# Parameter planes 0 to 3 of the S5 mixer, moved from the attention stage to the first feed-forward layer

## The reference, cut to what matters

```python
# first block, two layers
for layer in range(2):
    h = rms_norm(x, mix_pre_g[layer])
    m = pool_mixer(...) if layer == 0 else swa_sink_attention(q, kk, vv, sinks) @ w_o     # planes were made here
    x = x + rms_norm(m, mix_post_g[layer])
    f = conv_glu_ffn(rms_norm(x, ffn_pre_g[layer]), w_in, conv_w, conv_b, w_out)          # now in that of layer 0
    x = x + rms_norm(f, ffn_post_g[layer])
# second block: modulated norm, S5 mixer, MLP, then norm, SSD mixer, MLP, final norm
def _s5_mixer(h, w_in, lam_re, lam_im, log_dt, b_re, b_im, c_re, c_im, d, w_glu, b_glu):
    dt = exp(log_dt)[:, None]
    lam_bar = exp(lam * dt)                                    # complex, 64 groups x 64 states
    b_bar = ((lam_bar - 1) / lam)[..., None] * (b_re + i b_im) # 64 x 64 x 16
    c_mat = c_re + i c_im
    ...                                                        # scan over time, y = C h
```

## Time and profile before

| | |
|---|---|
| runs of the kernel before | 2322.3 us median, 2322.2 to 2325.84 (3 runs) |
| profiled execution | span 2324.2 us, the time that the page gives for it |
| PE busy | 99% of the span |
| DVE, ACT, POOL busy | 63%, 45%, 15% |
| PE's granted clock over 40 slices | 9 tenths or more in each |
| DMA, mean | 122 GB/s |

### The profile page before, as it was taken

One profiled execution on the slowest core, in us unless ns is written; L12 is line 12 of the kernel. 1 busy time (PEld: TensorE's weight loads), 2 busy tenths in 40 slices (PEclk: granted clock), 3 DMA queues, 4 the chain that ended last, 5 costly groups with the idle time before them and its releaser, 6 DMA issues. The chain is left out here.

```text
span 2324.2 us, 35082 instructions
## 1 busy us (share of the span) xinstructions
PE 2291.4 (99%) x12994; PEld 1930.6 (83%) x12994; DVE 1474.5 (63%) x2160; ACT 1051.7 (45%) x1728; POOL 348.9 (15%) x379
## 2 busy tenths in 40 slices
PE   9999999999999999999999999999999999999998
PEld 8888888867888888897788888888878789888888
DVE  5785788798688768879554324447578744432433
ACT  6653554556565344654344313325556533421421
POOL 0120121111322212110010000010136621000001
PEclk9999999999999999999999999999999999999999
DMA  5455453232345555544222222223212122232221
GB/s 216 143 183 197 174 184 124 82 116 73 137 168 178 186 167 185 179 186 165 71 77 106 91 106 93 91 82 110 95 56 76 39 91 91 91 106 93 90 93 70
DMA packets 56333, 282.53 MB, mean 122 GB/s; under 512 B 7980, under 2 KB 18992, under 8 KB 28320
## 3 DMA queue, kind: packets, MB, share of 16 engines
q1 hardware_dynamic: 34128, 213.85, 25.8%
q0 software_dynamic: 12560, 58.80, 7.4%
q10 hardware_dynamic: 9536, 8.39, 1.1%
HBM read 265.15 MB, written 15.86 MB: 121 GB/s over the span
## 5 line engine op out<-in xcount | busy, mean ns | idle before, releaser
L2329 DVE TENSOR_TENSOR w_lo<-raw,w_hi 128x1024 fp32r<-128x1024 f32 x386 | 505.4, 1346 | 399.8 <-ACT w_hi L1439 399.6
L1439 ACT ACTIVATE w_hi<-raw 128x1024 fp32r<-128x1024 f32 x386 | 388.8, 1053 | 416.1 <-PE ps L527 401.9
L525 PE MATMUL ps<-h_hi,w_hi 128*128 128x512 f32 (+1 forms) x1304 | 459.6, 352 | 5.2 <-DVE h_lo L2402 1.8
L526 PE MATMUL ps<-h_lo,w_hi 128*128 128x512 f32 (+1 forms) x1304 | 452.1, 347 | 1.6 <-issue 1.6
L527 PE MATMUL ps<-h_hi,w_lo 128*128 128x512 f32 (+1 forms) x1304 | 451.8, 346 | 0.0
L525 PEld LDWEIGHTS ps<-h_hi,w_hi 128*128 128x128 f32 x1304 | 246.9, 189 | 47.8 <-issue 11.3
L526 PEld LDWEIGHTS ps<-h_lo,w_hi 128*128 128x128 f32 x1304 | 247.0, 189 | 32.7 <-issue 2.6
L527 PEld LDWEIGHTS ps<-h_hi,w_lo 128*128 128x128 f32 x1304 | 247.1, 189 | 30.5
L531 PE MATMUL ps<-h_hi,w_hi 128*128 128x512 f32 (+1 forms) x712 | 270.6, 382 | 0.8 <-DVE tv L2828 0.8
L532 PE MATMUL ps<-h_lo,w_hi 128*128 128x512 f32 (+1 forms) x712 | 270.2, 382 | 0.0
L3430 POOL TENSOR_TENSOR sqsum<-sqsum,sq 128x256 f32<-128x256 f32 (+1 forms) x83 | 91.4, 1101 | 958.1 <-issue 588.8
(11 more groups left out here) (463 smaller groups left out, 3490.2 us busy)
## 6 DMA issues: line engine op xcount, KB each, us to landing
raw<-weights_dram SPq DMA_DIRECT2D x161, 1024.0 KB, 4.8
ada_w<-ada_dram POOLq DMA_DIRECT2D x48, 1024.0 KB, 5.1
raw<-weights_dram SPq DMA_DIRECT2D x32, 704.0 KB, 4.0
par<-par_dram SPq DMA_DIRECT2D x8, 1152.0 KB, 6.9
par_dram<-plane POOLq DMA_DIRECT2D x10, 512.0 KB, 3.8
tab<-tab_dram SPq DMA_DIRECT2D x8, 512.0 KB, 7.5
x_tok<-x_rows_dram SPq DMA_DIRECT2D x4, 512.0 KB, 5.5
x<-x_in_dram SPq DMA_DIRECT2D x1, 2048.0 KB, 14.5
```

The lines of the kernel that those rows point to most:

```text
L525: nc.tensor.matmul(dst, w_hi[:, o:o + P], rhs_hi, start=start, stop=False)
L526: nc.tensor.matmul(dst, w_hi[:, o:o + P], rhs_lo, start=False, stop=False)
L1439: nc.scalar.activation(w_hi[:, o:o + TILE // 2], raw[:, o:o + TILE // 2], ACT.Copy).then_inc(w_hi_done, 1)
L2329: nc.vector.tensor_tensor(w_lo[:, o], raw[:, o], w_hi[:, o].bitcast(f32), SUB).then_inc(w_split, 1)
```

## The change

Planes 0 to 3 are now made by DVE in `ffn0_out_b`: two pieces ahead of tile 0, then 3, 3, 3, 3 and 2 pieces behind `split_lo` in tiles 0 to 4 (`PIECES_BEFORE`, `PIECES_AT`). They lie, with their inputs and products, in the memory of `h_hi` and `h_lo`, which is idle in that phase. The constants that they need move one phase group earlier: `constants5` now runs in `ffn0_out_a`, in tiles 2, 4, 5 and 6, and ACT's `decay_functions` in tile 0 of it. Plane 4 stays in attention, in units 8 to 11, in buffers of its own. The stores of planes 0 to 3 are issued by ACT, behind its `squares`; those of plane 4 by POOL, as before. POOL loads `s5_b` and `s5_c` and zeroes the four buffers before its adds of `ffn0_out_b`. DVE waits for the eight stores before `stream_halves(0, ...)`, which overwrites the memory.

```diff
-    PLANE_PIECES = [(n, piece) for n in (1, 2, 3, 4) for piece in range(4)]
+    LAST_PLANE = 4
+    b_h, c_h, prod_h, cross_h = (place(n, D, offset=H0 + 4 * k * KB) for k, n in enumerate(("s5_b_early", "s5_c_early", "prod5_early", "cross5_early")))
+    plane5 = [[place(f"plane{u}{k}", D, offset=H0 + (16 + 8 * u + 4 * k) * KB) for k in range(2)] for u in range(2)]
+    PLANE_PIECES = [(n, piece) for n in range(LAST_PLANE) for piece in range(4)]
+    PIECES_BEFORE, PIECES_AT = 2, (3, 3, 3, 3, 2, 0)
...
# ACT
+        def planes_stored(s):
+            for n, part in parts_of(pieces_by(s - 1) if s else 0, pieces_by(s)):
+                o = (C_AT + (n - 1) * 2 * P if n else B0_AT) + part * P
+                act.wait_ge(sem("plane_im" if part else "plane_re"), n + 1)
+                act.dma_start(par_dram.rearrange("(j p) c -> p j c", p=P)[:, :, o:o + P],
+                              as3(plane5[n % 2][part][:, :], DC)).then_inc(sem(f"plane_stored{n % 2}"), 16)
         def rope_sines(s):
+            planes_stored(s)
...
-                if layer == 0 and half == "b":
-                    decay_functions()
-                    tiles(f"ffn{layer}_out_a", copy_out, (out_chunk, 1), then=transposed5 if layer else None)
+                    tiles(f"ffn{layer}_out_a", copy_out, (out_chunk, 1), then=transposed5 if layer else decay_functions)
...
# DVE
+            for u in range(2):
+                dve.wait_ge(sem(f"plane_stored{u}"), 64)
             stream_halves(0, post, {...
...
         def constants5(s):
-            if s == 0:
+            if s == 2:
                 lambda5()
-            elif s == 1:
+            elif s == 4:
                 powers5()
-            elif s == 2:
+            elif s == 5:
                 coefs5((1, 2))
-            elif s == 3:
+            elif s == 6:
                 coefs5((3, 4))
...
+        def early_planes5(s):
+            for piece in PLANE_PIECES[pieces_by(s):pieces_by(s + 1)]:
+                early5(*piece)
...
-                    tiles(f"ffn{layer}_out_a", nothing, ada=ADA_OUT[layer], then=fold5 if layer else None)
+                    tiles(f"ffn{layer}_out_a", nothing, ada=ADA_OUT[layer], then=fold5 if layer else constants5)
...
-                    tiles(f"ffn{layer}_out_b", add_out, (out_chunk, 1), splits="last", then=more_turns5 if layer else constants5, last=2)
+                    else:
+                        dve.wait_ge(sem("b_landed"), 16)
+                        dve.wait_ge(sem("c_landed"), 16)
+                        for piece in PLANE_PIECES[:PIECES_BEFORE]:
+                            early5(*piece)
+                    tiles(f"ffn{layer}_out_b", add_out, (out_chunk, 1), splits="last", then=more_turns5 if layer else early_planes5, last=2)
...
# DVE in attention
-        dve.wait_ge(sem("b_landed"), 16)
-        for piece in range(4):
-            early5(0, piece)
...
-            early5(*PLANE_PIECES[2 * s - 6])
             weigh(s - 3)
-            early5(*PLANE_PIECES[2 * s - 5])
             soften(s - 2)
...
-            if 8 <= j < 14:
-                early5(*PLANE_PIECES[j + 2])
+            if 8 <= j < 12:
+                early5(LAST_PLANE, j - 8)
...
# POOL
+                if half == "b" and not layer:
+                    gp.wait_ge(tile_done, tile_at(FIRST["ffn0_out_b"] - 1))
+                    gp.dma_start(b_h[:, :], s5_b).then_inc(sem("b_landed"), 16)
+                    gp.dma_start(c_h[:, :], s5_c).then_inc(sem("c_landed"), 16)
+                    for u in range(2):
+                        for k in range(2):
+                            ins = gp.memset(plane5[u][k][:, :], 0.0)
+                    ins.then_inc(sem("pool_set"), 1)
```

More of the change, by code:

```diff
@@ L102 @@
 START = {"mod_kept": 1, "xbc_done": 3}
-POOL_SET = {name: k + 1 for k, name in enumerate(("ones", "planes", "s5", "rows180", "rows181"))}
+POOL_SET = {name: k + 1 for k, name in enumerate(("ones", "planes", "last_plane", "s5", "rows180", "rows181"))}
 def eight(name, n=8):
@@ L229, in build, with pieces_by, parts_of @@
     small = place("small", 32 * 32, offset=W0)
[L230 to L233, removed]
-    PLANE_PIECES = [(n, piece) for n in (1, 2, 3, 4) for piece in range(4)]
-    def prod_of(n):
-        return prod5[min(n, 1)]
+    c_c = place("s5_c", D, offset=A0 + 16 * KB)
+    last_plane5 = [place(f"last_plane{k}", D, offset=A0 + (32 + 4 * k) * KB) for k in range(2)]
+    last_prod5, last_cross5 = place("last_prod5", D, offset=A0 + 56 * KB), place("last_cross5", D, offset=A0 + 60 * KB)
+    LAST_PLANE = 4
[3 more added lines that the diff above has]
+    PIECES_BEFORE, PIECES_AT = 2, (3, 3, 3, 3, 2, 0)
+    def pieces_by(s):
+        return PIECES_BEFORE + sum(PIECES_AT[:s])
+    def parts_of(lo, hi):
+        return [(n, piece // 2) for n, piece in PLANE_PIECES[lo:hi] if piece % 2]
     b_again = place("b_again", D, offset=A0 + 28 * KB)
@@ L1865, in _ @@
         act.wait_ge(sem("tables_landed"), 48)
-        act.wait_ge(sem("pool_set"), POOL_SET["planes"])
+        act.wait_ge(sem("pool_set"), POOL_SET["last_plane"])
         nc.scalar.activation(unit_r[:, :], ident[:, :], ACT.Copy)
@@ L2003, in _ @@
         g.after(6)
[L2004 to L2005 removed]
+        act.wait_ge(sem("last_plane_stored"), 32)
         ffn(1)
@@ L2996, in _ @@
                 output_lo(j)
-            if 8 <= j < 14:
-                early5(*PLANE_PIECES[j + 2])
+            if j == 8:
+                dve.wait_ge(sem("c_landed"), 32)
+            if 8 <= j < 12:
+                early5(LAST_PLANE, j - 8)
             if j in (8, 9, 10, 11, 12, 13):
@@ L3525, in _, with last_stored5 @@
         gp.wait_ge(tile_done, tile_at(FIRST["vproj"]))
-        gp.dma_start(b_c[:, :], s5_b).then_inc(sem("b_landed"), 16)
         gp.dma_start(c_c[:, :], s5_c).then_inc(sem("c_landed"), 16)
-        for u in range(2):
-            for k in range(2):
-                ins = gp.memset(plane5[u][k][:, :], 0.0)
+        for t in last_plane5:
+            ins = gp.memset(t[:, :], 0.0)
         ins.then_inc(sem("pool_set"), 1)
-        gp.wait_ge(sem("pool_set"), POOL_SET["planes"])
-        def store5(n, part):
-            o = (C_AT + (n - 1) * 2 * P if n else B0_AT) + part * P
-            gp.wait_ge(sem("plane_im" if part else "plane_re"), n + 1)
+        gp.wait_ge(sem("pool_set"), POOL_SET["last_plane"])
+        def last_stored5(part):
+            o = C_AT + (LAST_PLANE - 1) * 2 * P + part * P
+            gp.wait_ge(sem("plane_im" if part else "plane_re"), LAST_PLANE + 1)
             gp.dma_start(par_dram.rearrange("(j p) c -> p j c", p=P)[:, :, o:o + P],
-                         as3(plane5[n % 2][part][:, :], DC)).then_inc(sem(f"plane_stored{n % 2}"), 16)
-        for n in range(4):
-            for part in range(2):
-                store5(n, part)
+                         as3(last_plane5[part][:, :], DC)).then_inc(sem("last_plane_stored"), 16)
         zero(C["norm"].n)
@@ L3546, in _ @@
         for part in range(2):
-            store5(4, part)
+            last_stored5(part)
         ada_load()
```

32 lines of the change are left out of this document (16 added, 16 removed).

## The result

The changed kernel takes 2326.92 us (median of 20 runs, 2324.56 to 2329.7), the kernel before 2323.52 us (median of 20, beside it): the ratio is 1.0015, with a 95% interval of 1.0009 to 1.0021. That is 3.4 us more (2.1 to 4.9), less than 0.2%, but not nothing: the interval leaves out 1. One of the 20 runs of before, 3468.87 us, was in a slower state; without it the median is 2323.32 us, and the other 19 lie between 2322.01 and 2326.4 us. The forecast was 2326.7 us. The profiled execution took 2327.91 us, with a span of 2326.2 us: the time of a run is 1.7 us above its span. By that, before's profile, with a span of 2324.2 us, is of an execution of about 2325.9 us, well above before's median.

A forecast was written before the change was run, and what follows sets the result against it. PE, busy for 99% of the span, was taken to bound the kernel. Stall +4.2, attention -1.1 and clock +1.3 gave +4.4 us on a median of 2322.3: 2326.7 us, range 2321.5 to 2330.5.

The forecast's parts named there:

- Pieces against constants: In ffn0_out_b, 21.9 us of pieces replace 16.1 us of constants, so DVE reaches tile 5's add 5.8 us later.
- What PE sees: At out_pair, 5.8 us of DVE lateness less 1.6 us of slack gives 4.2 us of new waiting on PE.
- the last split: The split_lo for tile 7 in out_pair, with 1.57 us of slack, alone sets PE's total loss.
- the cross-check: PE's new waits at out_pair, taken singly: 1.0 and 0.5, then 2.2, then 0.5 us, again 4.2 in sum.
- Loads, memsets, stores, constants: Early loads, memsets and ACT's stores are hidden, and constants fit in ffn0_out_a: cost nothing.
- The rule that I had weighed for the memsets: GpSimd memsets read no SBUF, so they don't lock out DVE's a_lo; otherwise up to 0.9 us more.
- Attention: PE's wait for DVE's weigh near 487 us goes when pieces leave attention: -1.1 us, bounds 0.9 to 2.0.
- The clock: After the new PE idle time, 3.4 us at 1.2 GHz, costing +1.3 us (0 to 3.4).
- The rival with 6.7 us: The clock stays low twice as long, 6.7 us at half speed costing 3.4 us: about 2330 us, chance 0.20.
- an execution without a fall only for the new one, as a rival: Stall hidden, attention pauses before 522 us shrink and the clock stays up there: -1.1 - 3.4, 2317.8 us, chance 0.07.
- The sum: +4.2 - 1.1 + 1.3 = +4.4 us: 2326.7 us for the median, 2328.6 us for the span.
- The rival without a fall: The stall at out_pair comes but the clock stays up: +4.2 - 1.1, 2325.4 us, chance 0.18.

The follow-up runs named there:

- the doses: Kernel before with eight, or four, unused chained DVE operations between tile 4's split and tile 5's add in ffn0_out_b: 2328.35 us, or 2325.4 us.
- the half dose: Kernel before with four unused chained DVE operations between tile 4's split and tile 5's add in ffn0_out_b: 2325.4 us, ratio 1.0008.
- the constants alone: Kernel before with only the constants and their ACT functions moved to ffn0_out_a, pieces staying in attention: 2322.79 us, ratio 0.9998.
- its control: Kernel after with 13 calls of unused PE products, nine in pauses near 576 and 582 us, four in the output projection: 2325.34 us.
- the filled version: Kernel after with 13 unused PE products while PE waits for tile 7's bank: 2324.55 us, ratio 1.0007.
- the pieces in pauses: Kernel after with plane 3's four pieces moved from ffn0_out_b into DVE's pauses in out_pair: 2321.66 us, ratio 0.9995.
- both controls: Unused PE products near 576 and 582 us and in the output projection: 15 calls on kernel before, 2322.79 us; 13 on kernel after, 2325.34 us.
- all together: Kernel after with plane 3's pieces in DVE's pauses of out_pair and unused PE products in pauses around 515 us: 2319.9 us, ratio 0.9986.

## Why the prediction was right, by its steps

**Pieces against constants.** Forecast 5.8 us late, measured 5.6. The small difference is the one that the bounds named: a piece not followed directly by its partner takes 1.2 us.

**What PE sees.** Forecast 4.2 us, measured 3.7. The prediction's total hung on the last split, with a slack of 1.57 us; the trace has no wait there. The bank decided, with the 1.8 to 1.9 us that the doses and the change measured: 5.6 - 1.9 = 3.7. Reading a slack as the time from the end of one instruction to the start of the next one overstated it by 0.2 us here (2.06 at the bank, 1.57 at the split). Why the last split dropped out can be seen at 405.35: from there PE ran at half speed and came to the ninth chunk 1.4 us later, and the split, done at 408.5, was in time. With the half dose, where the clock stayed up, its 0.4 us are there. The partial waits of the cross-check (1.0 + 0.5, 2.2, 0.5) were 0.5 + 0.2, 2.1 and 0 in the view of waits. By starts, which count all, they were 0.6 + 0.4, 2.3 and 0, and 0.3 to 0.4 at tile 5, which the cross-check didn't have: tile 3's add comes behind 11 pieces and is 1.4 us late (389.66 against 388.68, and 0.4), a little more than the slack of its bank.

**Loads, memsets, stores, constants.** Forecast nothing, measured nothing: no wait of DVE for any of them, and the constants alone make no difference. The rule that I had weighed for the memsets (the Trainium skill, "SBUF — State Buffer", two separate sides) holds in this second row too: `a_lo` takes 0.69 us beside four of them.

**Attention.** Forecast -1.1, measured -1.1 in the trace; swapping two lines does it alone.

**The clock.** Forecast one fall of 3.4 us costing 1.3, measured one of 3.4 us costing 1.4. That rests on the kernel after and its control, with a fall there each, and on the filled version without one. The rival with 6.7 us was not this kernel's, but it was that of one pause of 3.8 us. Missed: I read the fall at 522 us in before's profile as a property of the kernel. It is there in only four of the ten traces in which PE's work is unchanged there (before, the pieces in pauses, and both controls). I had allowed for an execution without a fall only for the new one, as a rival.

**The sum.** 3.7 - 1.1 + 1.4 = 4.0 us from the trace, forecast 4.4, measured 3.4 between medians (2.1 to 4.9) and 2.0 between the two profiles. The rival without a fall (2325.4) lies inside the run-to-run spread; what speaks against it is the 0.87 in after's row and in its control's. The steps were the right ones, and of the trace's sum the stall was sized 0.5 us too large. That the forecast of 2326.7 us lies within 0.3 us of 2326.92 is luck, though: it stood on a median of 2322.3 us from three runs, where twenty give 2323.52, so a base 1.2 us too low made up for a change 1.0 us too large. The forecast of the span, 2328.6 us, was 2.4 us too high; 1.5 us of that are before's fall at 522 us, which after's execution didn't have.

Open: what makes the pause at 1070 us come and go. That it goes when 26 or 30 instructions are added to PE's program ahead of it is shown by five traces against seven; whether it is their number that counts, and whether it is the fetching of the program, was not tested.

## What to carry to other kernels

When work is moved onto an engine that is off the critical path, find the one place where the critical engine waits for it next, and read the slack from the trace (when is the result done, when is it wanted); lateness beyond it passes through in full. The remedy is then not to move less but to put the last part behind that hand-over, into the other engine's own pauses. Before crediting a gain to an edit, look at places that the edit can't reach: if they differ too, run a control with the same instruction count, and see in its trace that the added instructions run where they were meant to.

## What the runs showed of the hardware

In `out_pair` a pause of TensorE of 0.9 us left the clock at 2.4 GHz (one trace), 2.1 us, with 0.5 and 0.2 us ahead of it, was followed by 3.4 us at 1.2 GHz (two traces of two), and 3.8 us by 6.8 us (one trace). Elsewhere it is a matter of the execution: the 1.6 us at 1070 us brought a fall in three traces of seven, the group around 520 us in four of ten. A fall can also follow pauses of 0.6 us and less: there is one of 3.4 us at 1005 us with the half dose, at 1563 us in the kernel with all together (0.83 in 1560 to 1570) and at 1568 us in the control on after, and each of the last two cost 1.5 us. So the length of one pause doesn't decide alone. And removing a fall can give back less than its length at half speed, because other engines catch up during it: at 522 us 2.8 us were gained and 1.3 lost again within ten microseconds.

A pause of 1.6 us with no releaser stood in all seven traces with PE's program unchanged in length and in none of five with 26 or 30 instructions more, wherever ahead of it these were put (404 to 608 us). It cost 1.9 us.
